# A hybrid pool/conv encoder layer with MoE: conv chunk 1 moved to VectorE, equal projection blocks, last down product before the overflow loop

## The chip, the cores and the metric

The kernel runs on 1 core of one Trainium2 chip. The metric is the device time of one execution in microseconds (us), lower is better. The kernel before takes 1081.49 us, the median of 3 runs (1080.42 to 1083.44).

## The reference, cut to what matters

One inference step of one layer on 1024 prompt tokens and 64 sample tokens (T = 1088), all in float32, D = 1024:

```
z = rms_norm(x) @ w_in                         # 1024 -> 1536 columns
pool, value, gate = z[:, :512], z[:, 512:1024], z[:, 1024:]
y_pool = (trailing mean over 2/4/8/16 tokens - token) @ pool_lin[group] * pool_scale
v = value * sigmoid(gate)
h = causal depthwise conv of v, width 31, one filter per channel, + bias
y_conv = swish(layer_norm(h))                  # mean and variance over the 512 conv channels
x += concat(y_pool, y_conv) @ w_out + b_out
x += hier_moe(rms_norm(x))                     # 32 experts, two per token: (silu(x@Wg) * (x@Wu)) @ Wd
y = rms_norm(x) * norm_f_g                     # and the last rows of pool input and of v as new state
```

Channels beyond tokens: the 512 conv channels are four chunks of 128 (one channel per partition). An expert gets a block of 128 token slots; an expert with more tokens gets further blocks, the overflow blocks.

## The kernel before, in words

Each float32 product is made of three fp32r matmuls: an operand is split by ScalarE (ACT, the rounded high part, a Copy to fp32r) and VectorE (DVE, the low part, a subtraction), and TensorE (PE) adds high*high, high*low and low*high (`product`, L826 to L832).

**Input projection and mixers.** The 1088 token columns of the normalised, transposed x lie in SBUF. Twelve chunks of 128 output channels are projected one after another (`KINDS`, L313: gate 0, value 0, gate 1, value 1, ..., value 3, then pool 3 to pool 0). `in_proj(j, n)` (L845) works through three token blocks, 512, 512 and 64 wide (`BLOCKS`, L56), each 8 k-tiles times 3 matmuls. The result lies in one of two sets of three PSUM banks (`z_ps`). For each chunk the weights go through SP's load (`load_w_in`), ACT's `w_high(j)` (L571), DVE's `w_low(j)` (L1160); projection j waits for `wl_done`, and for the reader of the set of banks that it overwrites (`gate`, L610, `glu`, L1179, `pool_in`, L616).

**Convolution.** Chunk 0 (`TAPPED`, L66) is convolved on DVE: `taps(n)` (L1195) does n of the 31 taps, each as two instructions (parts A, 512 wide, and B, 606 wide) that multiply a shifted view of v by the tap's column and add. Chunks 1 to 3 (`PHASED`) are convolved on PE: `glu` writes v in four token phases, SP moves it by 16 small DMAs (`to_phases`, L423) into a layout with 32 channels by 4 phases on the partitions, PE runs 4 groups of 9 banded matmuls of 280 columns (`convolve`, L864), ACT evicts each group (`evict`, L625), SP moves it back (`from_phases`, L433). A table sets after which projection a chunk is convolved: `CONV_AFTER = {5: 1, 7: 2, 8: 3}` (L322). The order on DVE is written out by hand in L1261 to L1297: which `w_low`, `glu`, how many `taps`, `windows` (trailing sums of the pooling mixer), `ln_center`, `ln_normal` follow each other. `conv_done` is raised after the last tap; PE waits for it before `ln_mean(0)` (L877), which comes after projection 9. SP's queue is in order too: L441 to L463 interleave weight loads, band loads, `to_phases` and `from_phases`.

**Output projection, router and experts.** `out_proj`, router and planning follow (L968 to L1044), then a loop over 16 pairs of experts (`pair_loop`, L364; `body` on every engine). A pair is 12 weight pieces of 1 MB through 6 slots; the second down product of a pair is done inside the next pair's body (`EARLIER`, L343).

**End.** `pair_loop` holds a second loop over the overflow pairs, 8 turns whose body is skipped if there is no such pair. The trace shows 64 loads each of `w_eg`, `w_eu` and `w_ed`, that is 32 experts in halves, so no overflow block exists for these inputs. After that loop stand, on every engine, the last pair's second down product: SP loads its two pieces (L533 to L535), ACT evicts the pair's first result, converts the last hidden rows (`hidden_high`) and then the two pieces (L806 to L810), DVE makes the low parts (L1542 to L1545), PE multiplies (L1130). The result is scattered by POOL to `y2_dram` (L1700), POOL counts `sc_all` (L1705), SP loads the rows back (`load_y2`, L546), DVE and ACT combine and normalise nine token tiles (L1564), and SP stores them.

## Time and profile before

| | us |
|---|---|
| median of 3 runs | 1081.49 |
| the profiled execution | 1083.56 |
| its span in the profile | 1081.3 |
| busy in the span: PE, DVE, ACT, POOL | 977.4, 798.5, 587.8, 170.8 |
| mean granted clock of PE | 0.942 |

The sums of the prediction are made against the profiled execution. PE's shares are an average over stages: the projections and mixers (to some 300 us), output projection and router (to some 420), the expert loop (some 450 to 1010), and the end without PE. The two lines of the page that show this cut the span into 40 slices of 27 us; a digit is the busy share in tenths, PEclk is the granted clock in tenths of full speed:

```
PE   4999999999899995589999999999999999999810
PEclk8999999999899995689999999999999999999865
```

### The profile page before, as it was taken

The page shows a single profiled execution, that of the slowest core. Times are in us where ns is not written, and L with a number is a line of the kernel's source. Part 1 is how long each engine was busy: PE and PEld are TensorE (multiplying, and loading weights), DVE is VectorE, ACT ScalarE, POOL GpSimd, SP SyncE. Part 2 cuts the span into 40 slices and gives each one's busy share as a digit, 9 for nine tenths or more (in the row PEclk, how much of TensorE's full clock was granted, in tenths as well). Part 3 has the DMA queues.
Part 4 walks back from the last instruction along what each step waited for, and adds up shares of the span by engine and source line. Part 5 has one row for each costly group of instructions (what it writes and reads, how often), then busy time and mean ns, then how long its engine had stood idle before and what let it go on. Part 6 is the DMA issues. An engine that isn't in the chain of part 4 may idle for free. (4 is left out here: it accounts for less than half of the span.)

```text
span 1081.3 us, 13914 instructions
## 1 busy us (share of the span) xinstructions
PE 977.4 (90%) x4654; PEld 805.3 (74%) x4654; DVE 798.5 (74%) x872; ACT 587.8 (54%) x555; POOL 170.8 (16%) x210
## 2 busy tenths in 40 slices
PE   4999999999899995589999999999999999999810
PEld 3788888776688875478888888888888888888600
DVE  6374530336767868689898988989898989898548
ACT  7211110125643213368787787878787878787323
POOL 2000000000000002215222222223222222222100
PEclk8999999999899995689999999999999999999865
DMA  8411324211333224589999999999999999999766
GB/s 260 127 43 42 108 63 127 87 62 39 119 118 131 104 89 175 209 306 390 382 385 392 385 395 387 403 392 386 395 383 391 374 393 372 401 375 352 279 269 240
DMA packets 73067, 279.23 MB, mean 258 GB/s; under 512 B 17375, under 2 KB 33247, under 8 KB 47369
## 3 DMA queue, kind: packets, MB, share of 16 engines
q1 hardware_dynamic: 63241, 260.94, 63.9%
q0 software_dynamic: 9792, 17.85, 4.3%
q8 instruction: 20, 0.33, 0.1%
q14 instruction: 14, 0.11, 0.0%
HBM read 261.69 MB, written 31.38 MB: 271 GB/s over the span
## 5 line engine op out<-in xcount | busy, mean ns | idle before, releaser
L1487 DVE TENSOR_TENSOR big<-arena,big 128x2048 fp32r<-128x2048 f32 x128 | 286.7, 2278 | 0.0
L753 ACT ACTIVATE big<-arena 128x2048 fp32r<-128x2048 f32 x128 | 238.0, 1910 | 0.3 <-DMA arena<-in_w_eg 0.3
L1063 PE MATMUL ps<-big,ring 128*128 128x512 f32 x512 | 204.7, 400 | 2.4 <-DVE ring L1492 2.4
L1065 PE MATMUL ps<-big,ring 128*128 128x512 f32 x512 | 201.9, 394 | 0.0
L1064 PE MATMUL ps<-big,ring 128*128 128x512 f32 x512 | 201.3, 393 | 0.0
L1487 DVE TENSOR_TENSOR slot_tail<-arena,slot_tail 128x2048 fp32r<-128x2048 f32 x64 | 143.4, 2281 | 1.1 <-ACT slot_tail L753 1.1
L753 ACT ACTIVATE slot_tail<-arena 128x2048 fp32r<-128x2048 f32 x64 | 119.2, 1919 | 3.1 <-DVE eob L1472 3.1
L1063 PEld LDWEIGHTS ps<-big,ring 128*128 128x128 f32 x512 | 97.5, 191 | 22.3 <-DVE ring L1492 2.8
L1065 PEld LDWEIGHTS ps<-big,ring 128*128 128x128 f32 x512 | 97.2, 190 | 21.1
L1064 PEld LDWEIGHTS ps<-big,ring 128*128 128x128 f32 x512 | 97.4, 190 | 19.6
L1078 PE MATMUL ps<-slot_tail,hTr 128*128 128x512 f32 x256 | 103.4, 404 | 5.4 <-DVE slot_tail L1487 5.4
L829 PE MATMUL ps<-big,ring 128*128 128x512 f32 (+1 forms) x288 | 104.6, 363 | 0.4 <-DVE big L1157 0.4
L830 PE MATMUL ps<-big,ring 128*128 128x512 f32 (+1 forms) x288 | 102.3, 355 | 0.0
L831 PE MATMUL ps<-big,ring 128*128 128x512 f32 (+1 forms) x288 | 102.1, 356 | 0.0
L1080 PE MATMUL ps<-slot_tail,hTr 128*128 128x512 f32 x256 | 100.6, 393 | 0.0
L1079 PE MATMUL ps<-slot_tail,hTr 128*128 128x512 f32 x256 | 100.5, 393 | 0.0
L1492 DVE TENSOR_TENSOR ring<-ps,ring 128x1024 fp32r<-128x1024 f32 x32 | 39.2, 1224 | 58.4 <-ACT ring L757 58.4
L1654 POOL DMA_INDIRECT y_scratch<-arena,cur x32 | 74.5, 2329 | 26.3 <-POOL cur L1678 25.5
L757 ACT ACTIVATE ring<-ps 128x1024 fp32r<-128x1024 f32 x32 | 32.9, 1027 | 76.6 <-PE ps L1052 76.6
L829 PEld LDWEIGHTS ps<-big,ring 128*128 128x128 f32 x288 | 55.2, 192 | 9.7 <-issue 1.3
L830 PEld LDWEIGHTS ps<-big,ring 128*128 128x128 f32 x288 | 55.2, 192 | 9.3 <-issue 1.3
L1225 DVE TENSOR_TENSOR arena<-arena 128x1117 f32<-128x1117 f32 (+3 forms) x10 | 13.2, 1319 | 65.9 <-ACT arena L623 65.7
(229 smaller groups left out, 1476.9 us busy)
## 6 DMA issues: line engine op xcount, KB each, us to landing
arena<-in_w_eg SPq DMA_DIRECT2D x64, 1024.0 KB, 7.4
arena<-in_w_eu SPq DMA_DIRECT2D x64, 1024.0 KB, 8.4
arena<-in_w_ed SPq DMA_DIRECT2D x64, 1024.0 KB, 8.6
arena<-in_x_prompt SPq DMA_DIRECT2D x16, 512.0 KB, 4.2
arena<-y_scratch SPq DMA_DIRECT2D x8, 1024.0 KB, 11.3
arena<-in_conv_band SPq DMA_DIRECT2D x12, 576.0 KB, 4.2
arena<-in_w_in SPq DMA_DIRECT2D x12, 512.0 KB, 4.5
arena<-in_w_out SPq DMA_DIRECT2D x8, 512.0 KB, 4.5
```

The costliest lines, as they stand in the source:

```text
L753: act.activation(we_h[n % SLOTS], raw[n % RAWS], ACT.Copy).then_inc(high_done, 1)
L829: pe.matmul(out, sh, mh, start=(i == 0), stop=False)
L830: pe.matmul(out, sh, ml, start=False, stop=False)
L831: ins = pe.matmul(out, sl_, mh, start=False, stop=(i == len(parts) - 1 and last))
L1063: pe.matmul(out, part_h[b][:, k, :], wh[:, i, :], start=(k == 0), stop=False)
L1064: pe.matmul(out, part_h[b][:, k, :], wl[:, i, :], start=False, stop=False)
L1065: ins = pe.matmul(out, part_l[b][:, k, :], wh[:, i, :], start=False, stop=(k == KD - 1))
L1078: pe.matmul(out, hT_h[:, k, :], wh[:, i, c0:c0 + BANK], start=(k == 0), stop=False)
L1079: pe.matmul(out, hT_h[:, k, :], wl[:, i, c0:c0 + BANK], start=False, stop=False)
L1080: ins = pe.matmul(out, hT_l[:, k, :], wh[:, i, c0:c0 + BANK], start=False, stop=(k == KF - 1))
L1487: dve.tensor_tensor(we_l[n % SLOTS], raw[n % RAWS], we_h[n % SLOTS].bitcast(F32), ALU.subtract).then_inc(low_done, 1)
L1654: pool.indirect_dma_start(out=y2_dram, out_offset=bass.IndirectOffsetOnAxis(ap=at, axis=0), in_=ye[b], in_offset=None, bounds_check=last_r ...
```

## The change

Four things. (1) `TAPPED` becomes chunks 0 and 1: chunk 1 is convolved on DVE by 31 taps like chunk 0, and the DVE order is written anew; PE convolves chunks 2 and 3 alone, SP's queue is rearranged accordingly. (2) The projection takes three token blocks of 364, 364 and 360 columns, each in its own PSUM bank; the readers `gate`, `glu` and `pool_in` follow that layout with one or two instructions more. (3) The last pair's second down product uses slots 0 and 1 (`LAST`), is loaded right behind the pairs' loads, its ACT and DVE halves stand before the last hidden rows, its matmuls before the overflow loop; the overflow loop gets a body of its own. (4) SP loads the residual tiles 4 to 8 before 0 to 3 and waits for the scatters itself. `ln_sd` of the second LayerNorm block now shares its place with the first's, so ACT waits for `nrm_done` before `ln_deviation(1)`.

```
+    IW = -(-T // 12) * 4
+    IN_BLOCKS = [(n * IW, min(IW, T - n * IW)) for n in range(3)]
-    TAPPED, PHASED = (0,), (1, 2, 3)
+    TAPPED, PHASED = (0, 1), (2, 3)
-        ln_sd = [r_p[:, 0:BANK], r_p[:, BANK:2 * BANK], r_p[:, 2 * BANK:2 * BANK + DEC]]
+        ln_sd = [r_p[:, 0:BANK], r_p[:, 0:BANK], r_p[:, BANK:BANK + DEC]]
+        z_in = [z.rearrange("p (n w) -> p n w", n=3) for z in z_ps]
-        CONV_AFTER = {5: 1, 7: 2, 8: 3}
+        CONV_AFTER = {7: 2, 8: 3}
+        LAST = {0: 4, 1: 5}
...
         @block.sync
-            for j in (4, 5, 6, 7):
+            for j in (4, 5, 6, 7, 8, 9):
                 load_w_in(j)
             to_phases(0)
-            load_w_in(8)
+            load_w_in(10)
+            load_w_in(11)
             for k in range(GPC):
                 load_band(k + 3)
                 from_phases(k)
             to_phases(1)
-            load_w_in(9)
-            load_w_in(10)
-            for k in range(GPC, 2 * GPC):
-                load_band(k + 3)
-                from_phases(k)
-            to_phases(2)
-            load_w_in(11)
-            for k in range(2 * GPC, NGR):
+            for k in range(GPC, NGR):
...
+            pair_loop(sp, weights, 1)
+            for s, n in LAST.items():
+                sp.wait_ge(low_done, after(PAIRS - 1, s + RAWS))
+                load_piece(s, PIECES[n], {-1: E - 1})
+            n_pairs = over_loop(sp, over_weights)
...
-            sp.wait_ge(sc_all, 1)
+            sp.wait_ge(scat[0], 16 * n_pairs + 16)
+            sp.wait_ge(scat[1], 16 * n_pairs + 16)
...
         @block.scalar
-                act.activation(sg, z_ps[J["gate", c] % 2][:, 0:T], ACT.Sigmoid).then_inc(sg_done, 1)
+                z = z_in[J["gate", c] % 2]
+                act.activation(sg[:, 0:2 * IW].rearrange("p (n w) -> p n w", n=2), z[:, 0:2, 0:IW], ACT.Sigmoid)
+                act.activation(sg[:, 2 * IW:T], z[:, 2, 0:T - 2 * IW], ACT.Sigmoid).then_inc(sg_done, 1)
...
+            pair_loop(act, body, 1)
+            for s in LAST:
+                act.wait_ge(raw_in[s], 16 * (2 * PAIRS + 1))
+                act.wait_ge(piece_used, after(PAIRS - 1, s + SLOTS))
+                act.activation(we_h[s], raw[s], ACT.Copy).then_inc(high_done, 1)
+            result(PAIRS - 1, 0)
+            hidden_high(PAIRS - 1, 1)
+            result(PAIRS - 1, 1, end=True)
+            over_loop(act, over_body)
...
         @block.tensor
-                tok, w = BLOCKS[n]
-                ins = product(z_ps[j % 2][:, tok:tok + w],
+                tok, w = IN_BLOCKS[n]
+                ins = product(z_in[j % 2][:, n, 0:w],
...
+            pe.wait_ge(h_low, 2 * PAIRS + 2)
+            pe.wait_ge(ye_done, 2 * PAIRS + 1)
+            for s, n in LAST.items():
+                pe.wait_ge(low_done, after(PAIRS, n, end=True))
+                down(s, PIECES[n][2])
+            over_loop(pe, over_body)
...
         @block.vector
             glu(0)
-            taps(2)
+            taps(0, 2)
             w_low(3)
-            taps(7)
+            taps(0, 7)
             w_low(4)
-            taps(2)
+            taps(0, 4)
             glu(1)
             w_low(5)
-            taps(3)
+            taps(0, 7)
             w_low(6)
-            taps(4)
+            taps(0, 6)
             glu(2)
-            taps(1)
             w_low(7)
-            taps(6)
+            taps(0, TAPS - 26)
+            taps(1, 2)
             w_low(8)
-            taps(4)
+            taps(1, 10)
             glu(3)
             w_low(9)
-            taps(TAPS - 29)
+            taps(1, 12)
+            windows(3)
+            w_low(10)
+            taps(1, TAPS - 24)
             dve.wait_ge(conv_step, steps[0])
             dve.engine_nop().then_inc(conv_done, 2)
-            windows(3)
-            w_low(10)
             windows(2)
...
+            pair_loop(dve, body, 1)
+            for s, n in LAST.items():
+                dve.wait_ge(high_done, after(PAIRS, n, end=True))
+                dve.tensor_tensor(we_l[s], raw[s], we_h[s].bitcast(F32), ALU.subtract).then_inc(low_done, 1)
+            hidden(PAIRS - 1, 1)
+            hidden_low(PAIRS - 1, 1)
+            over_loop(dve, over_body)
```

Three places where instructions move. DVE around the last taps, where L1203 is a tap, L1225 to L1233 the windows of pool 3, L1283 the step that raises `conv_done`; before:

```order
L1162 TENSOR_TENSOR ring<-arena,ring 128x1024 [waits wh_done]
L1203 SCALAR_TENSOR_TENSOR arena<-arena,cols 128x512 [waits conv_step]
L1203 SCALAR_TENSOR_TENSOR arena<-arena,cols 128x606 [waits conv_step]
L1203 SCALAR_TENSOR_TENSOR arena<-arena,cols 128x512 [waits conv_step]
L1203 SCALAR_TENSOR_TENSOR arena<-arena,cols 128x606 [waits conv_step]
L1283 ISA [waits conv_step]
L1225 TENSOR_TENSOR arena<-arena 128x1117 [waits u_done]
```

and in the change, where the tap is L1296, the windows L1318 to L1326, the weights' low part L1246:

```order
L1296 SCALAR_TENSOR_TENSOR arena<-arena,cols 128x606 [waits conv_step]
L1318 TENSOR_TENSOR arena<-arena 128x1117 [waits u_done]
L1318 TENSOR_TENSOR arena<-arena 128x1115 [waits win_step]
L1318 TENSOR_TENSOR arena<-arena 128x1111 [waits win_step]
L1318 TENSOR_TENSOR arena<-arena 128x1103 [waits win_step]
L1321 TENSOR_TENSOR arena<-arena,inv_cnt 128x15 [waits win_step]
L1322 TENSOR_TENSOR arena<-arena 128x15 [waits win_step]
L1324 SCALAR_TENSOR_TENSOR arena<-arena 128x1103 [waits win_step]
L1326 COPY arena<-arena 128x15 [waits win_step]
L1246 TENSOR_TENSOR ring<-arena,ring 128x1024 [waits wh_done]
L1296 SCALAR_TENSOR_TENSOR arena<-arena,cols 128x512 [waits conv_step]
L1296 SCALAR_TENSOR_TENSOR arena<-arena,cols 128x606 [waits conv_step]
```

The windows of pool 3 and `w_low(10)` stood behind the last tap; now seven taps of chunk 1 stand behind them, and `conv_done` behind those.

SP's queue between the last two chunks convolved on PE (L438 and L461 are `from_phases`, L430 and L453 `to_phases`); before:

```order
L438 DMA arena<-arena 32x280 [waits ev_done]
L438 DMA arena<-arena 32x280 x3
L430 DMA arena<-arena 32x288 [waits cv_done,v_done]
L430 DMA arena<-arena 32x288 x15
L399 DMA arena<-in_w_in 128x8x128 [waits wl_done]
L421 DMA arena<-in_conv_band 128x1152 [waits cv_done]
```

and in the change:

```order
L461 DMA arena<-arena 32x280 [waits ev_done]
L461 DMA arena<-arena 32x280 x3
L453 DMA arena<-arena 32x288 [waits v_done]
L453 DMA arena<-arena 32x288 x15
L444 DMA arena<-in_conv_band 128x1152 [waits cv_done]
```

The weight load that followed is gone from there; the 16 DMAs of `to_phases` still stand behind the evictions of the chunk convolved before.

ACT at the end of the expert loop (before: L753 the pieces' high parts, L773 a result's eviction, L767 the hidden rows' high part, L371 and L372 the overflow loop):

```order
L371 COMPARE_AND_BRANCH
L771 ISA
L772 REGISTER_ALU [waits piece_used]
L773 ACTIVATE arena<-ps 128x1024 [waits scat0]
L765 ISA
L767 ACTIVATE hTr<-ps 128x512 [waits piece_used,h_tr]
L751 ISA
L358 REGISTER_ALU [waits raw_in4]
L753 ACTIVATE slot_tail<-arena 128x2048 [waits piece_used]
L753 ACTIVATE slot_tail<-arena 128x2048 [waits piece_used,raw_in5]
```

and in the change (L858 the pieces, L799 the evictions, L793 the hidden rows, L393 to L395 the overflow loop):

```order
L388 COMPARE_AND_BRANCH
L858 ACTIVATE big<-arena 128x2048 [waits piece_used,raw_in0]
L858 ACTIVATE big<-arena 128x2048 [waits piece_used,raw_in1]
L799 ACTIVATE arena<-ps 128x1024 [waits scat0,piece_used]
L793 ACTIVATE hTr<-ps 128x512 [waits piece_used,h_tr]
L799 ACTIVATE arena<-ps 128x1024 [waits scat1,piece_used]
L393 TENSOR_LOAD eob [waits plan_done]
L395 COMPARE_AND_BRANCH
```

The two pieces stand before the last result's eviction and the hidden rows, and the overflow loop behind everything.

## Rows read from the trace of the kernel before

**Rows 1.** Stretches (A:B in us): busy us per engine, granted clock, DMA share, GB/s

```profile
50.00:100.00 50.00, 50.00 (x268) 43.04 (x266) 27.74 (x36) 4.15 (x4) 2.33 (x4) 1.00 0.16 44
...
500.00:600.00 100.00, 100.00 (x474) 83.21 (x473) 91.22 (x53) 79.94 (x61) 25.96 (x23) 1.00 0.98 385
...
1040.00:1082.00 42.00, 0.00 (x0) 0.00 (x0) 35.50 (x36) 14.17 (x28) 0.00 (x0) 0.50 0.77 299
```

**Rows 2.** Timeline of PE, second projection: start, duration, instruction, shape, records merged

```profile
46.30 0.48 PE L829 MATMUL ps<-big,ring 128*128 128x512 f32 x1
...
51.39 0.39 PE L830 MATMUL ps<-big,ring 128*128 128x512 f32 x1
...
57.29 0.19 PE L829 MATMUL ps<-big,ring 128*128 128x64 f32 x1
...
59.88 0.48 PE L829 MATMUL ps<-big,ring 128*128 128x512 f32 x1
```

**Rows 3.** Timeline of PE: the router's matmuls, 36 columns wide

```profile
321.59 1.87 PE L1002 MATMUL ps<-w_rt,arena 128*128 128x36 f32 x16
```

**Rows 4.** Timeline of PE and ACT: start and last eviction of chunk 1's convolution

```profile
114.23 6.14 PE L873 MATMUL ps<-arena 128*128 128x280 f32 x25
...
131.50 0.49 ACT L628 ACTIVATE arena<-ps,b_ph 128x280 f32<-128x280 f32 x1 [3.75 <-PE ps L873]
```

**Rows 5.** Timeline of ACT, SP and PE around chunk 3's convolution

```profile
175.67 0.49 ACT L628 ACTIVATE arena<-ps,b_ph 128x280 f32<-128x280 f32 x1 [3.75 <-PE ps L873]
...
178.70 11.13 SPq L430 DMA_DIRECT2D arena<-arena  x16
...
191.21 9.03 PE L873 MATMUL ps<-arena 128*128 128x280 f32 x30 [2.06 <-DMA arena<-arena]
```

**Rows 6.** Stretch behind that wait, columns as in rows 1

```profile
191.00:195.00 4.00, 3.79 (x9) 2.84 (x10) 3.90 (x4) 0.42 (x1) 0.00 (x0) 0.57 0.47 131
```

**Rows 7.** Timeline of PE: LayerNorm's mean, flat (L883) and phased (L885) chunks

```profile
223.97 1.02 PE L883 MATMUL ps<-arena,mean_w 128*128 128x512 f32 x2
224.83 5.39 PE L885 MATMUL ps<-arena,mean_w 128*128 128x512 f32 x6
```

**Rows 8.** Timeline of DVE: first taps, 14 tap instructions, GLU, weights' low part, windows

```profile
61.55 1.06 DVE L1206 TENSOR_SCALAR arena<-arena,cols 128x512 f32<-128x512 f32 x2
...
65.07 10.05 DVE L1203 SCALAR_TENSOR_TENSOR arena<-arena,cols 128x512 f32<-128x512 f32 x14
...
158.67 1.99 DVE L1185 TENSOR_TENSOR arena<-ps,arena 128x1024 f32<-128x1024 f32 x1 [4.68 <-PE ps L831]
...
190.51 5.37 DVE L1225 TENSOR_TENSOR arena<-arena 128x1117 f32<-128x1117 f32 x4 [25.83 <-ACT arena L623]
...
197.76 1.22 DVE L1162 TENSOR_TENSOR ring<-arena,ring 128x1024 fp32r<-128x1024 f32 x1
```

**Rows 9.** Timeline of ACT, DVE and PE at the end of the expert loop

```profile
1017.22 0.60 PE L1087 MATMUL ps<-ident,arena 128*128 128x128 f32 x4
...
1018.42 0.59 ACT L767 ACTIVATE hTr<-ps 128x512 fp32r<-128x512 f32 x1
...
1019.04 0.69 DVE L1506 TENSOR_TENSOR hTr<-ps,hTr 128x512 fp32r<-128x512 f32 x1 [5.83 <-ACT hTr L767]
...
1023.19 0.80 PE L1078 MATMUL ps<-slot_tail,hTr 128*128 128x512 f32 x1 [5.37 <-DVE slot_tail L1487]
...
1030.58 0.39 PE L1080 MATMUL ps<-slot_tail,hTr 128*128 128x512 f32 x1
```

**Rows 10.** The chain that ended last: start us, us, what

```profile
1033.18 3.20 DMA y_scratch<-arena,cur
...
1036.43 4.72 DMA arena<-y_scratch
```

**Rows 11.** Stretch in the last down product, columns as in rows 1

```profile
1023.00:1028.00 5.00, 4.81 (x12) 3.82 (x13) 2.33 (x2) 0.00 (x0) 0.00 (x0) 0.54 0.91 302
```

More of the change, by code:

```diff
@@ L1058, in expert_in, with gate_up @@
                 pe.wait_ge(low_done, after(j, n))
+                gate_up(n, b, half, out)
+            def gate_up(n, b, half, out):
                 wh = we_h[n % SLOTS].rearrange("p (k n) -> p k n", n=FF)
@@ L1066, in expert_in, with expert_out, down @@
                 ins.then_inc(piece_used, 1)
-            def expert_out(j, n, end=False):
-                half = PIECES[n][2]
-                pe.wait_ge(low_done, after(j, n, end))
+            def expert_out(j, n):
+                pe.wait_ge(low_done, after(j, n))
+                down(n, PIECES[n][2])
+            def down(n, half):
                 wh = we_h[n % SLOTS].rearrange("p (k n) -> p k n", n=D)
@@ L1093, in earlier_down, with body @@
                 for n in EARLIER:
[L1094 removed]
+                    expert_out(j, n)
             turn_rows(0, 0, first=True)
[L1098 removed]
+            def body(j, first=False):
                 pe.wait_ge(xe_low, 2 * j + 1)
@@ L1126, in body, with over_body @@
                 turn_hidden(j, 1)
-            body(0, False, first=True)
-            n_pairs = pair_loop(pe, body, 1)
-            earlier_down(n_pairs, end=True)
+            def over_body(j):
+                for b in range(2):
+                    pe.wait_ge(xe_low, 2 * j + 1 + b)
+                    pe.wait_ge(silu_done, 2 * j + 2 + b)
+                    for n in range(2):
+                        pe.wait_ge(low_done, over(j, 6 * b + n))
+                        gate_up(n, b, n, gate_ps)
+                    pe.wait_ge(act_done, 2 * j + 2 + b)
+                    for n in range(2):
+                        pe.wait_ge(low_done, over(j, 6 * b + 2 + n))
+                        gate_up(2 + n, b, n, up_ps)
+                    turn_rows(j + b, 1 - b)
+                    turn_hidden(j, b)
+                    pe.wait_ge(h_low, 2 * j + 3 + b)
+                    pe.wait_ge(ye_done, 2 * j + 2 + b)
+                    for n in range(2):
+                        pe.wait_ge(low_done, over(j, 6 * b + 4 + n))
+                        down(4 + n, n)
+            body(0, first=True)
+            pair_loop(pe, body, 1)
+            pe.wait_ge(h_low, 2 * PAIRS + 2)
[4 more added lines that the diff above has]
+            over_loop(pe, over_body)
         @block.vector
@@ L1482, in _, with low @@
             slots(0, E)
-            def low(j, n, end=False):
-                dve.wait_ge(high_done, after(j, n, end))
+            def low(j, n):
+                dve.wait_ge(high_done, after(j, n))
                 dve.tensor_tensor(we_l[n % SLOTS], raw[n % RAWS], we_h[n % SLOTS].bitcast(F32),
```

262 lines of the change are left out of this document (157 added, 105 removed).

## The prediction

> **What bounds the kernel now.** I read the busy times by stretch first, then the timeline of the engine that is full in each stage, then the chain that ended last. In the projection stage TensorE is busy for 50.00 of 50 us and VectorE for 27.74 [rows 1]: a matmul taken away there moves the end, and VectorE has room. In the expert loop TensorE is busy for all of 100 us and the DMA engines for 0.98 [rows 1]; the change touches nothing in it. At the end no TensorE work is left and VectorE is busy for 35.50 of 42 us [rows 1]; the change leaves those instructions alone, so that only the moment counts at which the last scatter lands. The chain starts from that scatter and the load behind it [rows 10]. So I price TensorE's work in the projection stage, the cover for VectorE's added work, and the stretch from the last hidden rows to the last scatter. All are made against the profiled execution of 1083.56 us, 2.07 above the median of 1081.49.
>
> **Projection blocks.** One projection takes 59.88 - 46.30 = 13.58 us [rows 2]: 48 matmuls of 512 columns from 46.30 to 57.29 and 24 of 64 columns in the other 2.59, 0.108 each. The 26 full ones from 51.39 to 57.29 follow each other at 0.227 us. 512 columns at 2.4 GHz, the level of this stretch (granted clock 1.00), are 0.213, so a matmul costs its columns and 0.0135. The narrow ones are on a floor, not on their columns: the router's 36-column matmuls take (1.87 - 0.19)/15 = 0.112 each, 0.19 being the length of a short one [rows 2, 3], much the same as 64 columns. The change has 72 matmuls of 364 or 360 columns. By columns at 2.4 GHz plus 0.0135 each takes 0.165, the projection 11.9 us, 1.7 less. No row shows this width. Bound on one side: the 280-column matmuls of the convolution follow at (6.14 - 0.40)/24 = 0.239 each [rows 4], within 0.006 of two cycles a column; with that overhead 0.158 and 11.4, 2.2 less. Other bound: a straight line through 64 and 512 columns gives 13.58 again, since columns and matmuls are the same in number, and nothing is gained. I take 1.7, because the 36-column row shows that the floor does not rise with the width below 64, which the straight line needs.
>
> The Trainium skill, TensorE: Matmul & The Clock Gate, section Back-to-back issue gap, prices an isolated warm matmul at N/2.4 + 2.5 ns, which is 154 ns for 364 columns. By that figure, an estimate from the page, a projection would take 11.1 us and the sum below would be some 8.8 us smaller. The trace disagrees at 512 columns, 227 ns against the page's 216, so the measured overhead stands.
>
> Twelve projections would give 20.4. One does not count: chunk 3's convolution waits today for its phase layout, 2.06 us [rows 5]. SP issues those 16 copies, 11.13 us, only behind the evictions and copies of chunk 2; from chunk 2's last eviction at 175.67 to the start at 191.21 it takes 15.5 us, and this chain stays as it is. A projection of 11.9 in between leaves 3.7 us of waiting. So eleven count: 18.7 us. The half-speed stretch behind that wait (granted clock 0.57 in 191 to 195, about 1.7 us of work lost [rows 6]) I keep as it is.
>
> **Convolution.** Chunk 1 leaves TensorE: from 114.23 to its last eviction at 131.50, less the 0.05 to that eviction's start, 17.2 us [rows 4], in a stretch where TensorE is full. All of it counts: -17.2. Its 12 bands become 8 and its 32 copies go from SP's queue; nothing there was waited for except the layout above.
>
> **VectorE's added work.** 30 further tap pairs at 10.05/7 = 1.44 us and a first one of 1.06 [rows 8] are 44 us, less a phased GLU of 1.99 for a flat one of some 1.5. I cost it at nothing; the cover is TensorE. Count from the end of projection 1. VectorE must raise the flag behind the last tap: 60 x 1.44 + 2 x 1.06 = 88.5 of taps, some 7.4 of GLU, nine weight halves at 1.14 = 10.3, the windows of pool 3 of 197.76 - 190.51 = 7.25 [rows 8], together 113. TensorE asks for it after projections 2 to 9 (95), two convolutions (34.4), the wait and the slow stretch (5.4): 135. VectorE cannot run through: the windows need projection 8, which ends at 95 - 11.9 + 17.2 = 100.5, with some 1.5 for ScalarE. From there 7.25, 1.14 and seven tap pairs (10.1) end at 120.5, some 14 us early. Each earlier weight half comes out before its projection too; the tightest is the seventh, 51 against 59. GLU 3, behind the first twelve taps of chunk 1, is ready at 80, before chunk 2's convolution ends (88.6), so the SP chain is not later either. If a tap pair cost over 1.65 us this cover would be gone.
>
> **LayerNorm.** The mean's matmul of a flat chunk starts its successor 224.83 - 223.97 = 0.86 later; the three phased chunks take 5.39, 1.80 each [rows 7]. One phased chunk becomes flat in both 512-token blocks, and TensorE goes on from there with the next projection: -1.9. Centre and scale on VectorE get shorter by some 0.4 each, hidden beside projection 11; the wait of the second deviation for the first block's scaling is over before its time, since that scaling is ordered ahead of it on VectorE today. The further instructions in the readers of PSUM (one or two of 0.2 us each) lie beside TensorE.
>
> **The end.** Today TensorE turns the last hidden rows until 1017.82, ScalarE converts until 1019.01, VectorE until 1019.73, and only then come the two weight pieces; the product starts at 1023.19 after 5.37 idle and ends at 1030.97 [rows 9]. With the pieces ahead of the hidden rows it can start at 1019.8: 3.4 earlier. The pieces fit: both engines are idle before. Its 24 matmuls are 5.45 at full clock; today they take 7.78, since the clock is 0.54 from 1023 to 1028 [rows 11], 2.2 lost. Behind a 2 us wait I take the loss of rows 6, where as long a wait came ahead, 1.7: end at 1027.0, -4.0. Without any loss it is -5.7, with all of today's -3.4. The scatter (3.20) and the first load (4.72) [rows 10] then start that much earlier. Dropping POOL's count and loading the residual tiles in another order I cost at nothing: those loads are issued before 1024 in either, and not waited for.
>
> **Sum.** 18.7 + 17.2 + 1.9 + 4.0 = 41.8. 1083.56 - 41.8 = 1041.8 for the profiled execution, 1081.49 - 41.8 = **1039.7** for the median.
>
> **Rivals.**
> Straight line. If the load of weights is paid beside the columns in proportion, the projection stays at 13.58: +18.7, that is 1058.4. For it: the totals of columns and loads are unchanged. Against it: the like times at 36 and 64 columns. 6%.
>
> VectorE becomes the bound. If tap pairs cost 30% more with two chunks in turn, 1.87: the 55 pairs ahead of the windows end some 18 us late, GLU 3 some 12, so the last layout some 3 later than today, and the flag about 7 us behind TensorE. Some 1047. For it: the chain of stages has only 14 us to spare. Against it: nothing in the taps changes but addresses, and 14 of them ran at 0.72 each with both other engines at work. 6%.
>
> Slower than before: the full fp32r rate holds only for wider matmuls. 64 columns at four cycles are 0.107 us, which is also what the narrow ones take (0.108, rows 2); the trace cannot tell this from the floor. Should 364 columns go at that rate, 0.612 each, a projection takes 44 us, +30.5 twelve times: 366 more, less the 23 of the other terms, some 1424. It decides if the change of rate lies between 364 and 512 columns. Against it: nothing between them in the trace speaks for a limit there. 3%.
>
> No change: the instruction order shows the convolution gone from TensorE, so this is left for the case that waits give all of it back. 1%.
>
> **How the numbers follow.** The forecast has 84%. Its own bounds: projection 2.2 instead of 1.7 and no slow clock at the end, 1039.7 - 5.5 - 1.7 = 1032.5; half the projection gain missing, 1049. The range of 1033 to 1052 takes in that and VectorE's case, and leaves out the straight line and the slower rival. About 0.3% is what a measurement can tell from no change. Faster by more: forecast, straight line, VectorE, 96%; within: 1%; slower: 3%.
>
> **What would show it.** Matmuls of L829's successor 0.165 apart and projections 11.9 apart; no convolution between projections 5 and 6; a wait of 3.7 before the last convolution and no other of TensorE on VectorE up to the means; VectorE's last tap 10 to 15 us before the mean; the last down product starting some 2 us after the last turned rows. A gap of TensorE in front of a projection or the first mean, ended by VectorE, would prove the cover wrong; matmuls at 0.19 or more the width.

## The result, and the profile after the change

The changed kernel takes 1032.24 us (median of 4 runs, 1031.88 to 1032.66), the kernel before beside it 1081.14 (4 runs, 1080.42 to 1083.44): a ratio of 0.9545, 95% interval 0.9531 to 0.9558, 48.9 us less. The forecast was 1039.7 with a range from 1033.0: right in sign, 7.5 too high, and the result lies 0.8 below the range. The profiled execution took 1032.55 with a span of 1030.8; the spans are 50.5 apart.

The page's 40 slices of the changed kernel, now 25.8 us each: PE's busy tenths and its granted clock.

```profile
PE   4999999998999964899999999999999999999900
PEclk8999999999999956999999999999999999999955
```

Against the same two lines of before, the 8 and the 6 at the end of PEclk are gone: the last product no longer runs at half speed.

The timeline of PE in the changed kernel: second projection and start of the next, start of chunk 2's convolution, end of projection 9 with the means, last turned rows and last product.

```profile
42.73 0.33 PE L881 MATMUL ps<-big,ring 128*128 128x364 f32 x1
...
54.73 0.32 PE L881 MATMUL ps<-big,ring 128*128 128x364 f32 x1
...
126.59 1.10 PE L925 MATMUL ps<-arena 128*128 128x280 f32 x4
...
158.17 17.25 PE L925 MATMUL ps<-arena 128*128 128x280 f32 x72 [2.47 <-DMA arena<-arena]
...
187.66 1.88 PE L935 MATMUL ps<-arena,mean_w 128*128 128x512 f32 x4
189.38 3.64 PE L937 MATMUL ps<-arena,mean_w 128*128 128x512 f32 x4
...
242.57 0.71 PE L1034 MATMUL ps<-big,ring 128*128 128x512 f32 x1 [3.62 <-issue]
...
972.24 0.60 PE L1147 MATMUL ps<-ident,arena 128*128 128x128 f32 x4
974.73 0.50 PE L1138 MATMUL ps<-big,hTr 128*128 128x512 f32 x1 [1.89 <-DVE hTr L1600]
```

A projection is 54.73 - 42.73 = 12.00 for 72 matmuls, 0.167 each (before 13.58, [rows 2]). There is no convolution between projections 5 and 6. ScalarE's last eviction of chunk 2, SP's copies for chunk 3, and VectorE's last taps:

```profile
143.78 0.50 ACT L652 ACTIVATE arena<-ps,b_ph 128x280 f32<-128x280 f32 x1 [3.75 <-PE ps L925]
...
146.76 10.10 SPq L453 DMA_DIRECT2D arena<-arena  x16
...
165.51 10.05 DVE L1296 SCALAR_TENSOR_TENSOR arena<-arena,cols 128x512 f32<-128x512 f32 x14
```

The wait for chunk 3's layout is 2.47 (before 2.06, [rows 5]), the wait of the last product 1.89 (before 5.37, [rows 9]).

Cutting both timelines at the same places of the program gives where the 50.5 went; the third column is what of it is clock, that is, matmuls that ran at half speed in one trace and not in the other.

| stretch of TensorE | gain | of it clock |
|---|---|---|
| projection 0 | 3.55 | 1.7 |
| projections 1 to 7 | 11.38 | |
| chunk 1's convolution (0.08 of it in chunk 2's) | 16.94 | |
| projection 8, layout wait, chunk 3's convolution | 2.83 | 1.7 |
| projection 9 | 1.57 | |
| means, variances, projections 10 and 11, to the output projection | 5.31 | |
| output projection to the last turned rows | 3.38 | 3.4 |
| last turned rows to the end | 5.52 | 2.0 |
| sum | 50.48 | 8.8 |

The 3.4 ahead of the last turned rows is clock, net. 1.8 of it lie between the output projection and the first hidden rows, where the kernel before lost 3.1 to half speed and the changed one 1.5. The other 1.6 lie in the first expert pair, where it lost 2.9 and the changed one nothing, but a wait for VectorE that the kernel before does not have takes 1.16 back:

```profile
432.02 0.50 PE L1121 MATMUL ps<-big,ring 128*128 128x512 f32 x1 [1.16 <-DVE big L1581]
```

The change edits nothing in that stretch. Without the clock the sum is 41.7; the forecast's sum of 41.8 had 41.2 without its clock (of its 4.0 at the end, 0.6 is clock). So the arithmetic of the change held, and the surplus is clock, mostly behind waits that are there in both kernels. The experiments are about that.

The same stretch of the first expert pair in windows: span, busy us of PE, PEld, DVE, ACT and POOL, granted clock, DMA share, GB/s. First the kernel before, behind a wait of 3.34 us:

```profile
464.00:472.00 8.00, 6.65 (x20) 5.42 (x20) 7.74 (x13) 4.96 (x4) 0.07 (x1) 0.57 0.66 240
```

and the changed kernel, behind a wait of 3.33 us for the same thing:

```profile
421.00:429.00 8.00, 7.00 (x33) 5.88 (x34) 7.68 (x13) 4.92 (x5) 0.00 (x0) 1.00 0.80 289
```

20 matmul records at a clock of 0.57 against 33 at 1.00, in code that the change leaves alone. Below, a wait is said to pay when matmuls behind it run at half speed; what it pays is the work lost by that, in us.

### The profile page after: what moved, and what is told of

It reads as the page before. It is cut to its first block, busy times and chain, and to the rows that moved or that the text cites. A ratio compares the mean times of both kernels' runs of the same rounds, so it can differ in the third digit from the quotient of the medians.

```text
span 1030.8 us, 13764 instructions
## 1 busy us (share of the span) xinstructions
PE 929.1 (90%) x4582; PEld 787.4 (76%) x4582; DVE 838.2 (81%) x940; ACT 590.7 (57%) x559; POOL 162.6 (16%) x205
## 4 chain that ended last, share of the span: by engine, by line
PE 85%; DVE 6%; DMA 3%; issue 2%; ACT 2%; SPq 1%; POOLq 0%; DVEq 0%; POOL 0%; ACTq 0%
PE ps L1121 11%; PE ps L1123 11%; PE ps L1122 11%; PE ps L1138 6%; PE ps L1140 6%; PE ps L1139 6%; PE ps L881 4%; PE ps L882 4%; PE ps L883 4%; PE ps L925 3%; PE ps L1034 3%; PE ps L1035 3%; PE ps L1036 3%; PE ps L1107 3%; DVE arena L1669 2%
## 5 line engine op out<-in xcount | busy, mean ns | idle before, releaser
L779 ACT ACTIVATE big<-arena 128x2048 fp32r<-128x2048 f32 x128 | 243.2, 1915 | 14.7 <-DMA arena<-in_w_eg 12.0
L1581 DVE TENSOR_TENSOR slot_tail<-arena,slot_tail 128x2048 fp32r<-128x2048 f32 x62 | 139.1, 2286 | 0.0
L1121 PEld LDWEIGHTS ps<-big,ring 128*128 128x128 f32 x512 | 96.6, 189 | 23.3 <-DVE ring L1586 2.8
L1123 PEld LDWEIGHTS ps<-big,ring 128*128 128x128 f32 x512 | 96.5, 188 | 20.6
L1122 PEld LDWEIGHTS ps<-big,ring 128*128 128x128 f32 x512 | 96.7, 189 | 19.0
L1138 PE MATMUL ps<-slot_tail,hTr 128*128 128x512 f32 x248 | 99.2, 400 | 0.0
L881 PE MATMUL ps<-big,ring 128*128 128x364 f32 (+1 forms) x288 | 97.3, 338 | 0.0
L1140 PE MATMUL ps<-slot_tail,hTr 128*128 128x512 f32 x248 | 96.9, 391 | 0.0
L1139 PE MATMUL ps<-slot_tail,hTr 128*128 128x512 f32 x248 | 96.8, 390 | 0.0
L883 PE MATMUL ps<-big,ring 128*128 128x364 f32 (+1 forms) x288 | 95.0, 330 | 0.0
L882 PE MATMUL ps<-big,ring 128*128 128x364 f32 (+1 forms) x288 | 95.0, 330 | 0.0
L1296 DVE SCALAR_TENSOR_TENSOR arena<-arena,cols 128x512 f32<-128x512 f32 x120 | 86.2, 797 | 0.0
L1772 POOL DMA_INDIRECT y_scratch<-arena,cur x32 | 69.6, 2174 | 26.3 <-POOL cur L1796 24.7
L1034 PE MATMUL ps<-big,ring 128*128 128x512 f32 (+1 forms) x144 | 57.4, 399 | 3.6 <-issue 3.6
L1035 PE MATMUL ps<-big,ring 128*128 128x512 f32 (+1 forms) x144 | 56.8, 395 | 0.0
## 6 DMA issues: line engine op xcount, KB each, us to landing
arena<-y_scratch SPq DMA_DIRECT2D x8, 1024.0 KB, 11.3
```

The costliest lines, as they stand in the source:

```text
L779: act.activation(we_h[n % SLOTS], raw[n % RAWS], ACT.Copy).then_inc(high_done, 1)
L881: pe.matmul(out, sh, mh, start=(i == 0), stop=False)
L882: pe.matmul(out, sh, ml, start=False, stop=False)
L883: ins = pe.matmul(out, sl_, mh, start=False, stop=(i == len(parts) - 1 and last))
L1034: pe.matmul(out, sh, wo_h[:, k, c0:c0 + BANK], start=(i == 0), stop=False)
L1121: pe.matmul(out, part_h[b][:, k, :], wh[:, i, :], start=(k == 0), stop=False)
```

## The experiments

**Blocks alone.** The kernel before with `IN_BLOCKS` and its three readers:

```
-                tok, w = BLOCKS[n]
-                ins = product(z_ps[j % 2][:, tok:tok + w],
+                tok, w = IN_BLOCKS[n]
+                ins = product(z_in[j % 2][:, n, 0:w],
```

> The kernel before with the 364/364/360 blocks and their readers alone; convolution, SP's order and the end as before. Measured in the change, a projection takes 1.61 us less, so ten of them (projections 1 to 7 and 9 to 11) give 16.1, and projection 8 is eaten by the wait for chunk 3's layout, which grows from 2.06 to some 3.7. Projection 0 is the open part. Theory 'as priced' (a wait of some 2 us costs 1.7 of half-speed clock, whatever stands around it): projection 0 gives 1.6 too, 1081.1 - 17.7 = 1063.4, and the half-speed stretches of before at chunk 3's convolution, in the first expert pair and in the last down product are all still there. Theory 'narrow' (a wait costs clock where 64-column matmuls stand ahead of it): projection 0 gives 3.7 and the stretch behind the layout wait goes (1.7), 1059.6; first pair and last product stay slow. Theory 'moment' (the same wait pays or does not pay according to when it comes, so a shift of the program changes which waits pay): between 1055.5 and 1063.4, with one or two of the four stretches gone or come back without a change in what stands ahead of them, the two at the end included.

Measured 1059.79 (1059.22 to 1061.69), before beside it 1080.68: ratio 0.9806 (0.9788 to 0.9824), 20.9 less. The layout wait is 3.19, near the 3.7 forecast. In its trace projection 0, chunk 3's convolution and the first pair ran at full clock, the last product (wait 5.37) did not. 'As priced' falls. The time is the one that 'narrow' named (1059.6), but 'narrow' has the first pair slow, and the blocks cannot reach the pair: its full clock speaks for 'moment' and against 'narrow' as the whole cause.

**Narrow block first.** The kernel before:

```
-                for n in range(3):
-                    in_proj(j, n)
+                for n in (2, 0, 1):
+                    in_proj(j, n, end=1)
```

> The kernel before with the 64-column block of projections 1 to 11 computed first and the two 512-column blocks behind it: the same matmuls and the same moments at each projection's end, but wide matmuls ahead of the wait in front of chunk 3's convolution. Theory 'narrow': the 4 us behind that wait run at a granted clock of 1.00 instead of 0.57 and 1.7 us are gained, 1079.4; projection 0 is not changed and stays slow. Theories 'as priced' and 'moment': the wait comes at the same time and the stretch stays at 0.57, 1081.1.

Measured 1087.37 (1085.73 to 1088.73), 6.7 slower: none of the theories. Chunk 3's convolution was at full clock, but three new half-speed stretches stand in narrow blocks or right behind them: where projection 0's narrow block meets projection 1's, and in projections 10 and 11, whose narrow blocks follow the means. PE where projection 0's narrow block (42.90 on) meets projection 1's, and the windows there (columns as above):

```profile
42.90 0.19 PE L829 MATMUL ps<-big,ring 128*128 128x64 f32 x1
...
45.94 0.28 PE L830 MATMUL ps<-big,ring 128*128 128x64 f32 x1
46.05 0.34 PE L831 MATMUL ps<-big,ring 128*128 128x64 f32 x1
46.20 0.40 PE L829 MATMUL ps<-big,ring 128*128 128x64 f32 x1
46.42 0.40 PE L830 MATMUL ps<-big,ring 128*128 128x64 f32 x1
```

```profile
42.00:46.00 4.00, 4.00 (x34) 3.84 (x32) 0.00 (x0) 0.23 (x1) 0.00 (x0) 1.00 0.00 0
46.00:50.00 4.00, 4.00 (x21) 4.00 (x21) 0.79 (x1) 3.07 (x3) 0.00 (x0) 0.52 0.00 0
```

TensorE is busy for all of the 8 us and waits for nothing, yet the clock falls at about 46.1, in the second of two narrow blocks, and the matmuls follow at 0.213 instead of 0.111. So narrow matmuls can cost clock without any wait.

**Later start.** 40 no-operations on SP ahead of its first load, in the changed kernel and in the one before.

> The changed kernel with 40 no-operations on SP ahead of its first load, so that everything starts some 1 to 3 us later (the shift is read from the first load's issue) and nothing else changes. Theories 'as priced' and 'narrow': 1032.2 plus the shift, and the four places that were slow before the change (projection 0, chunk 3's convolution, first expert pair, last down product) run at a granted clock of 1.00 as they did unshifted. Theory 'moment': one or more of the four comes back at half speed, 1.6 to 2.2 us each, so the time is the shift plus 0 to 7.5.

> The kernel before with the same 40 no-operations ahead of SP's first load. Theories 'as priced' and 'narrow': 1081.1 plus the shift, with the four slow stretches as they are. Theory 'moment': at least one of the four goes, so the time rises by less than the shift or falls, down to the shift less 7.5.

The no-operations delayed nothing: the first load is issued at 0.78 in the changed kernel with and without them, at 0.80 in the other. Nor does anything hide ahead of the span: device time and span are 1.8 apart in the changed kernel and 2.2 in the other, with and without the no-operations. Both runs are repeats, and that is what makes them useful. The changed kernel took 1036.03 (1032.27 to 1037.74), the one before 1081.10 (1080.79 to 1082.74). In the trace of the repeated changed kernel the first pair has the same wait as in the first trace, and pays:

```profile
424.06 1.12 PE L1149 MATMUL ps<-ident,arena 128*128 128x128 f32 x4 [3.33 <-DVE arena L1595]
```

```profile
423.00:431.00 8.00, 6.94 (x21) 5.66 (x22) 7.71 (x14) 4.90 (x5) 0.00 (x0) 0.57 0.72 250
```

The repeated kernel before lacks the half-speed stretches in projection 0 and in the first pair that its first trace has. One program, two executions, different clock: 'moment' needs no shift of the program. I called the next theory 'draw': whether a wait pays is decided anew in each execution.

**The changed kernel again**, nothing edited.

> The changed kernel once more, nothing edited. The 40 no-operations turned out to delay nothing in the traced span (first load issued at 0.78 in either), so that run was in effect the changed kernel too and took 1032.3 to 1037.7, with 2.9 us of half-speed clock in the first expert pair that the first trace of the changed kernel lacks. Theory 'draw': whether a wait of TensorE costs half-speed clock behind it differs between executions of one and the same program; then the times spread over some 5 us from 1032, the median lies at 1033 to 1036, and the profiled execution shows half-speed stretches at other places than the first trace. Theory 'fixed by the program': 1031.9 to 1032.7 again and the same stretches.

1032.70, the five runs at 1032.02, 1036.92, 1032.47, 1037.11 and 1032.70. Over the three builds that are the changed kernel, 13 executions lie at 1031.88 to 1037.74 with a median of 1032.66; the four of the result lie in the lower part of that, and the five above 1033 all at 1035.68 or more. The profiled execution, 1032.02, has the same stretches as the first trace, and the median is below the 1033 to 1036 that 'draw' named; it is the other runs that decide. The two near 1037 have a mean granted clock of 0.947 and 0.945, the other three 0.950 to 0.952, and nothing was edited: 'fixed by the program' falls.

What each wait cost in the eleven traces without filling (PE's busy time times what the clock lacks to 1, in slices of 2 us):

| wait ahead of | length | paid in | each |
|---|---|---|---|
| last tile's transposes in projection 0 | 1.59 | 5 of 11 | 1.7 |
| chunk 3's convolution | 1.8 to 3.2 | 2 of 10 | 1.5, 2.9 |
| output projection | 3.6 to 3.9 | 11 of 11 | 1.5 to 3.1 |
| first hidden rows | 3.33 | 6 of 11 | 1.7 to 3.0 |
| last product, as changed | 1.89 | 2 of 6 | 1.7 |
| last product, pieces late | 5.4 | 5 of 5 | 2.1 to 2.5 |

**Layout first.** The changed kernel with chunk 3's copies earlier in SP's queue:

```
                 load_band(k + 3)
                 from_phases(k)
-            to_phases(1)
+                if k == 0:
+                    to_phases(1)
```

> The changed kernel with SP's 16 layout copies for chunk 3 issued behind the first group's copies of chunk 2 instead of behind all four. VectorE's GLU 3 is done at 134.4, so the 10.1 us of issue can run from there to some 144.5, 11 us before projection 8 ends. Theory 'the wait is SP's order': the 2.47 us wait before chunk 3's convolution goes, 1032.2 - 2.5 = 1029.8; VectorE's last tap (175.6) is then 9.6 instead of 12.1 ahead of the first mean and still costs nothing. Rival: the copies collide with the band loads and the wait is only moved to a band, less than 1 us gained. Under theory 'moment' the 2.5 us shift of all that follows can bring slow stretches back, first pair 1.6 and last product 2.2, so up to 1033.6.

SP's timeline and PE's start of chunk 3's convolution in this kernel:

```profile
137.16 10.70 SPq L453 DMA_DIRECT2D arena<-arena  x16
```

```profile
158.13 0.33 PE L884 MATMUL ps<-big,ring 128*128 128x360 f32 x1
158.29 2.05 PE L926 MATMUL ps<-arena 128*128 128x280 f32 x8
```

The wait is gone, so it was SP's order. The time is not: 1032.38 (1032.01 to 1037.04). The profiled execution, 1037.04, paid 1.7 in projection 0, 3.0 at the output projection, 2.8 in the first pair and 1.7 at the last product, 7.7 more than the first trace of the changed kernel. In the times a gain of 2.5 cannot be seen through draws of this size. The granted clocks suggest that it is there: at a mean clock of 0.945 to 0.949 three runs of this kernel take 1032.0 to 1032.4, where the changed kernel at 0.945 to 0.948 takes 1035.7 to 1037.7.

**Pieces late.** The changed kernel with the pieces' conversion behind the last hidden rows on ACT, and likewise on DVE:

```
+            result(PAIRS - 1, 0)
+            hidden_high(PAIRS - 1, 1)
             for s in LAST:
...
-            result(PAIRS - 1, 0)
-            hidden_high(PAIRS - 1, 1)
```

> The changed kernel with the two last weight pieces behind the last hidden rows again, on ScalarE and VectorE, as before the change; TensorE's order and slots stay. Theory of the prediction (the pieces' place is the whole gain at the end): TensorE waits 5.3 us instead of 1.9 for the last product, +3.4, and if the longer wait brings the half-speed clock back (2.2 lost before the change) +5.6: 1035.6 to 1037.8. Rival (the overflow loop behind the product and the waits on it were the cost): under +1, 1033.2 at most.

```profile
977.58 0.60 PE L1147 MATMUL ps<-ident,arena 128*128 128x128 f32 x4
983.56 0.77 PE L1138 MATMUL ps<-big,hTr 128*128 128x512 f32 x1 [5.38 <-DVE big L1661]
```

The wait is 5.38 and the clock's loss behind it is back (2.5). Measured 1043.02 (1037.58 to 1043.91). Above the forecast, because this profiled execution also paid 1.7 in projection 0, 3.0 in the first pair and 1.5 more at the output projection; between the fastest runs of the two, one run each, it is 1037.58 - 1031.88 = 5.7, the forecast 5.6, and in the trace 3.5 of wait and 2.5 of clock. The pieces' place is the gain at the end.

**Widths.** Blocks of 512, 416 and 160.

```
-    IN_BLOCKS = [(n * IW, min(IW, T - n * IW)) for n in range(3)]
+    IN_BLOCKS = [(0, 512), (512, 416), (928, 160)]
```

> The changed kernel with token blocks of 512, 416 and 160 columns, three reader instructions instead of two. The same columns and the same 72 matmuls in a projection. Theory 'columns plus a fixed part above a floor' (0.0135 us and 0.416 ns a column, not under 0.112): 0.227, 0.187 and 0.112, a projection 24 x 0.526 = 12.6 us, 0.65 longer than 364/364/360; eleven times, less what the layout wait takes back, +6.5: 1038.7. Rival straight line through 64 and 512 columns: 0.227, 0.201 and 0.134, a projection 13.5 us, +16: 1048. Without any floor 160 columns would take 0.080 and the projection 11.9, 1032.

PE in its third projection: the first and last matmul of each width, and the next projection.

```profile
58.08 0.43 PE L884 MATMUL ps<-big,ring 128*128 128x512 f32 x1
...
63.57 0.35 PE L884 MATMUL ps<-big,ring 128*128 128x416 f32 x1
...
67.86 0.35 PE L886 MATMUL ps<-big,ring 128*128 128x416 f32 x1
68.05 0.23 PE L884 MATMUL ps<-big,ring 128*128 128x160 f32 x1
...
70.58 0.28 PE L886 MATMUL ps<-big,ring 128*128 128x160 f32 x1
70.69 0.43 PE L884 MATMUL ps<-big,ring 128*128 128x512 f32 x1
```

416 columns take (67.86 - 63.57)/23 = 0.187, 160 take (70.58 - 68.05)/23 = 0.110, the projection 70.69 - 58.08 = 12.61: the 12.6 of the floor theory, and the straight line with its 13.5 falls. The time is 1045.33 (2 runs); the profiled execution took 1044.62 and paid 1.7 each in projection 0, in the first pair and at the last product, which the first trace of the changed kernel did not: 1039.5 without these, for 1038.7.

**More taps.** 16 tap pairs more behind chunk 1's last one.

```
+            for _ in range(16):
+                for part in ("A", "B"):
...
+                    dve.scalar_tensor_tensor(hc_tap[:, 1, a:b], v_tap[:, 1, a + 30:b + 30], gdif[:, 0, 0:1],
```

> The changed kernel with 16 further tap pairs on VectorE behind the last one of chunk 1, multiplied by a zero column, so that the values stay: 16 x 1.44 = 23.0 us more work ahead of the first mean. Theory 'VectorE has 12.1 us to spare' (last tap at 175.6, TensorE asks at 187.7): TensorE waits 11.0 us more, 1043.2 plus up to 2 of half-speed clock behind the wait. Rival 'the added taps had been paid already in slower neighbours': the time rises by near the whole 23, 1055. If something else covers it, under 5.

DVE's last work and PE's first mean:

```profile
177.71 22.85 DVE L1382 SCALAR_TENSOR_TENSOR arena<-arena,gdif 128x512 f32<-128x512 f32 x32
```

```profile
200.83 3.75 PE L935 MATMUL ps<-arena,mean_w 128*128 128x512 f32 x4 [10.76 <-DVEq L1387]
```

TensorE waits 10.76 (forecast 11.0): VectorE has 12.1 to spare in the changed kernel, and TensorE was the cover. 1047.85 is 15.6 over the result: 10.8 of wait, 2.9 of clock behind it and 1.7 in projection 0.

**Waits filled.** The changed kernel with the layout copies early, as in 'Layout first', and matmuls that nobody reads in four waits; then in the planning stage too.

```
+            def keep_on(out, n):
+                m = mean_w[:, :].unsqueeze(1).to_broadcast([P, 3, P])
+                for _ in range(n):
+                    pe.matmul(out.rearrange("p (c n) -> p c n", c=3), mean_w[:, :], m, start=True, stop=True)
```

> The changed kernel with the layout copies of chunk 3 behind the first group (no wait left before its convolution), and with matmuls whose results nobody reads put into four waits of TensorE, each shorter than the wait: 8 of 364 columns inside projection 0, 5 float32 ones of 384 columns ahead of the output projection, 4 ahead of the first hidden rows, 2 ahead of the last down product. Theory 'draw' (a wait may cost clock, a filled one does not): none of these four places shows half speed, the times lie within about 1 us, and the median is 1032.2 less 2.5 for the layout wait less 1.5 for the stretch at the output projection that the first trace of the change had, 1028.2. Rival 'the clock falls whatever TensorE does in the wait': as many half-speed stretches as in the other runs, 1030 to 1036, and spread over several us.

> As the run with filled waits, and the waits of the planning stage and of the first rows filled too (3, 3, 4, 2, 14 and 3 float32 matmuls of 384 columns, 0.65 each at full clock), where every trace so far shows TensorE at half speed for some 40 us. Theory 'draw': the 40 us run at full clock and the matmuls there that stand in the chain of planning and first expert rows halve: last router tile 1.7, transposes 0.5, tables 1.5, first rows 1.0, first expert matmuls 2 to 3, together some 5 on the path, 1023. Rival: the filling delays what waits behind it by as much (each group may overrun by up to 0.6, and at half speed takes twice as long), 1028 to 1035.

1030.61 (1030.03 to 1032.63) and 1028.00 (1027.25 to 1028.70), beside 1032.70 for the unfilled kernel on the same chip; against the kernel before 0.9543 (0.9529 to 0.9556) and 0.9513 (0.9500 to 0.9527). The windows of the first filled kernel at the output projection and in the first pair, then of the second in the planning stage:

```profile
238.00:246.00 8.00, 7.64 (x32) 5.56 (x31) 6.88 (x9) 7.33 (x11) 0.00 (x0) 1.00 0.35 133
418.00:426.00 8.00, 7.24 (x34) 5.56 (x33) 7.74 (x11) 5.11 (x4) 0.21 (x1) 1.00 0.72 262
```

```profile
364.00:404.00 40.00, 34.73 (x150) 23.86 (x151) 32.21 (x134) 11.93 (x11) 10.56 (x8) 0.87 0.48 174
```

None of the four waits paid in either trace, the output projection included, which paid in all eleven others. By this the first run's rival falls; by the times alone it would not, since 1030.03 to 1032.63 is in its range and wider than the 1 us that 'draw' named. The gains are smaller than forecast (2.1 and 4.7 us for 4.0 and 9.2). The first is the layout order's: the output projection starts 2.13 earlier than in the first trace of the changed kernel, but from there to the first hidden rows the filled kernel takes 179.06, and the changed kernel, in two traces with a loss of 1.5, takes 179.43 and 178.92. So a loss of 1.5 at the output projection is hardly time, and what filling does for a run is to spare it the draws. In the planning stage, half speed for some 40 us in the unfilled traces and 0.87 on the mean here, TensorE now waits 2.31 for VectorE and 0.88 for a gather, and two half-speed stretches are left, so the second run's rival, that the filling delays what stands behind it, is not excluded. The last kernel beats both the one before and the changed one.

**The kernel before, filled.** Its five waits filled (the fifth behind the overflow loop), then the first four only, then the fifth ahead of the overflow loop.

> The kernel before, with matmuls whose results nobody reads in its own five waits: 6 of 512 columns inside projection 0, and float32 ones of 384 columns, 3 ahead of chunk 3's convolution, 5 ahead of the output projection, 4 ahead of the first hidden rows, 8 ahead of the last down product. Nothing else is changed. Theory 'the arithmetic was right and the clock was left out': between two kernels that both keep the clock, the change is worth the parts counted without clock, which the two traces give as 41.4, and the filled version of the changed kernel has no layout wait, 2.5 more; so 1030.6 + 41.4 + 2.5 = 1074.5, 6 below the kernel before, in a narrow band. Rival 'the change removed something else too' (fewer instructions, transfers earlier): the filled kernel before stays within 2 us of 1080.4 and the distance to the filled changed kernel is 48 to 50.

> The kernel before with its four waits ahead of the expert loop's second pair filled, and nothing at the end. The run with all five filled reached the last turned rows at 1010.78 instead of 1017.22; from there the kernel before takes 66.3 to its end. Theory 'the clock is the rest': 1010.8 + 66.3 = 1077.1 if the last product draws the half-speed stretch, 1075.0 if not. Against the filled changed kernel (1030.6, which has no layout wait) that is a distance of 44.4 to 46.5, of which 41.4 is the arithmetic, 2.5 the layout order and 2.1 the last product's clock. Rival 'the filling costs as much as the clock it keeps': 1080 or more.

> As the former, with 7 float32 matmuls of 384 columns (4.55 us) behind the last turned rows and ahead of the overflow loop, in the 5.4 us that TensorE waits there for the last weight pieces. Theory: the last product runs at full clock, 1075.0. Rival: the overflow loop's own steps on TensorE take longer than the wait once they stand behind other work, as in the run with the filling behind the loop, where TensorE was busy with nothing for 9.15 us: then the product starts 4 to 8 us later and the time is 1079 to 1083.

1086.42, 1081.99 (ratio 1.0011, 1.0002 to 1.0020) and 1085.90: by their times the theories failed in all three. The second run falls to its rival (1080 or more), the other two lie above what theory and rival named. The traces say where. None of the first four waits paid, and the last turned rows start at 1010.78, 1011.44 and 1012.05 instead of 1017.22. Behind them the second of these kernels does this (PE, then DVE's weight pieces):

```profile
1011.44 0.60 PE L1100 MATMUL ps<-ident,arena 128*128 128x128 f32 x4
1021.60 0.79 PE L1091 MATMUL ps<-slot_tail,hTr 128*128 128x512 f32 x1 [9.56 <-issue]
```

```profile
1015.06 4.49 DVE L1503 TENSOR_TENSOR slot_tail<-arena,slot_tail 128x2048 fp32r<-128x2048 f32 x2 [1.10 <-ACT slot_tail L753]
```

The second piece is done by 1019.6 at the latest, yet TensorE starts at 1021.60 and waits for nothing that the engines' rows show. Between stands the overflow loop; in the kernel before TensorE was through it within the 5.37 us of its wait [rows 9]. Why TensorE is idle for 9.2 and 9.6 there in two of these builds, and for 7.9 behind the filling in the third, is open: their code for TensorE is longer by some dozens of instructions, and little else was edited. One difference stands in the DMA tables, between the last turned rows and the product, first in the kernel before (1018 to 1023.19), then in the second of these (1012 to 1022):

```profile
q8 instruction: 1, 0.02, 1.2%
```

```profile
q8 instruction: 2, 0.03, 1.3%
```

Each counts loads of instructions (queue, kind: loads, MB, share of the window). The kernel before has one more only after its product has started, between 1023.8 and 1024.5; the other two filled kernels have two ahead of it, as here. That TensorE waits for the second load is the nearest explanation, but no run tests it. Up to the last turned rows the comparison stands: against 969.72 in the first filled changed kernel the distance is 41.1 to 42.3, less 2.5 for the layout order 38.6 to 39.8. The table's parts without clock up to there give 38.2, the unfilled first traces 45.0.

## Why the prediction was right and wrong

**Projection.** Forecast 11.9, measured 12.00: the floor and the columns, as argued from [rows 2, 3]; 0.167 a matmul, not 0.165. By the figure of the Trainium skill, TensorE: Matmul & The Clock Gate, section Back-to-back issue gap, an estimate from the page, it would be 0.154; the trace disagrees. (In the prediction's sentence on it, what is 8.8 smaller is the time; the sum of the gains would be larger.)

**Convolution, means, VectorE.** 16.94 for 17.2 (I counted to the eviction, 0.4 behind the next projection's start), 1.8 for 1.9, and VectorE's last tap ends at 175.56, 12.1 ahead of the mean, for 14. Nothing of its added 44 us is seen. **Layout wait.** 2.47 for 3.7: the chain from chunk 2's last eviction took 14.4 instead of 15.5, one microsecond of it SP's 16 issues.

**The end.** Start 3.5 earlier for 3.4; in the trace no half speed behind it, which I had given a loss of 1.7.

**The step that failed** is the clock. "The half-speed stretch behind that wait (granted clock 0.57 in 191 to 195, about 1.7 us of work lost [rows 6]) I keep as it is", and at the end, "Behind a 2 us wait I take the loss of rows 6, where as long a wait came ahead, 1.7". Both take a half-speed stretch of one execution as a property of the program, and the other three waits of the kernel before that paid are left out of the sum, as if they would pay again. The repeats show it to be a draw: the same 3.33 us wait paid 2.9 in one execution of the changed kernel and nothing in two others. What decides the draw, no run shows. By the Trainium skill, TensorE: Matmul & The Clock Gate, section What's actually happening, what the chip watches runs freely and does not start with the kernel, so that the same kernel differs from run to run; the traces agree in that the same stretch ran at 0.57 in one and at 1.00 in another.

The sum was made against an execution that had paid at all five waits, 11.3 by the same count; 2.07 of that was taken off by going to the median. The changed kernel's four runs paid little, 1.5 at the output projection in the trace. That is 8.8 of the 50.5, and 0.6 was priced. A part of this is luck: of the 13 executions five lie at 1035.68 or above, inside the range. Not all of it is, since the forecast is above all 13. Some of it belongs to the change and will recur: a wait of 5.4 paid in all five traces that have it, one of 1.89 in two of six. The lower bound was worked out as 1032.5, with "no slow clock at the end" and a projection 2.2 instead of 1.7 shorter, and the range began at 1033.0. "No slow clock at the end" alone gives 1038.0; the shorter projection did not come, and the full clock at the other waits, which did, was not among the bounds.

Of the rivals none happened. The straight line is excluded by the widths, VectorE as the bound by the added taps, the slower rate by the 0.167 of the projection's matmuls.

## What to carry over

Take the half-speed stretches out of a profile before making a sum against it: count them wait by wait, price the change without them, and set the range from no draw to all of them. A change that only removes a short wait of TensorE can vanish in these draws; look at the granted clock of every run, or fill the waits first. Where narrow matmuls sit on a floor, here 0.11 us from 36 to 160 columns, equal blocks wide enough to lie above it cost their columns and a small part each, here 0.015.

## What was not expected of the hardware

TensorE's clock fell to half amid 64-column matmuls without a gap. Their floor follows the clock, 0.111 at full and 0.213 at half speed. The Trainium skill, TensorE: Matmul & The Clock Gate, section LDWEIGHTS (loading the stationary operand), gives the time of a weight load by its columns, for 128 of them 0.107, an estimate from the page: near what the trace shows at full speed and half of what it shows at half speed. That the floor is the weight load is not shown. Matmuls whose results nobody reads, put into waits of 1.6 to 3.8 us ahead of the expert loop's second pair in five traces and into the wait of 1.89 at the end in two, were followed by a clock of 1.00 each time. In the planning stage they raised it only to 0.87, and around the overflow loop of the kernel before half speed came all the same. Around the overflow loop, whose body is skipped, TensorE was idle for 9.2 and 9.6 us in two builds; the 5.4 of the kernel before in the same place are a wait for weight pieces.
